# Down-projections of six of eight MLP stretches as seven block products, in a one-core hybrid decoder layer

## The chip, the cores and the metric

One Trainium2 chip, one of its cores. The metric is the device time of one execution in microseconds (us). The kernel before was timed three times: median 2252.41, from 2246.67 to 2255.57. The engines are TensorE (PE, matmuls), VectorE (DVE), ScalarE (ACT), GpSimd (POOL), and SyncE (SP), which only issues transfers.

## The reference

One layer for 1024 prompt tokens and 8 x 8 sample tokens (T = 1088 columns), model width 1024. A combined input projection feeds a retention branch and an RWKV-7 branch; their outputs are gated, merged and projected (`w_out`), then comes cross-attention, then the MLP, then a final norm. The change is about the MLP and about what prepares its weights:

```python
x = x + merged @ w_out
hq = _rmsnorm(x, g_cross)                     # cross-attention: w_cq, scores, softmax, values, w_co
x = x + ox @ w_co
hm = _rmsnorm(x, g_mlp)
x = x + jnp.square(jax.nn.relu(hm @ w_up)) @ w_down   # w_up 1024 x 4096, w_down 4096 x 1024
y = _rmsnorm(x, g_final)
```

## The kernel before, in words

**Number format.** Each weight and activation is held as a high part in fp32r and a remainder (the "low" part); one product is three matmul passes, high x high, high x low, low x high. For a weight tile POOL casts the high part and, in the projections, also subtracts to get the low part (`split`, L449 and L451). In the MLP POOL only casts (`pair`, L509) and DVE subtracts (`unit_lo`).

**Slots.** All weights lie in DRAM as slots of 128 x 1024, numbered: 14 RWKV slots from S_PW, 32 side slots, 8 branch-mix slots from S_MIX, 8 output-projection slots from S_OUT, 8 query slots, 8 slots of `w_co`, and then 64 MLP slots. SP loads a slot into a ring of two, POOL splits it, PE runs 72 matmuls on it. POOL's program is in the order of the slots; behind each of the first 32 splits it issues one DRAM-to-DRAM transfer (`sum_step`), which builds sums and differences of blocks of `w_up` in `sums_up` (a copy, `put`, or an adding transfer, `plus`), waiting on the semaphore `d_sum` of its group before it builds on an earlier one. SP waits for all of them before the first MLP load.

**MLP.** The hidden width is cut into 8 stretches of 512 columns, two to a group: group o = 0, then 1 and 2 in a hardware loop of two trips, then 3 (`pair_loop`); d = 0 or 1 is the stretch within the group. A stretch has two quads. A quad computes 256 hidden columns as seven block products (a Strassen-like scheme) over 2 x 2 blocks: token half, and input-row half or hidden-column half. Each product is a unit: one 256 KB load into the ring `mraw` of four, one cast, one low part, and 24 matmuls of 272 columns on two PSUM banks (`product`, issued through L517). ACT and DVE combine the accumulators in `hidf`, apply ReLU and the norm (`squeezed`), square on ACT (`squared`, a high part into `hid` and a full one into `hidf`), and DVE takes the low part (`hidden_lo`). After two quads the down-projection of these 512 hidden columns follows in the plain way: eight output tiles, each a unit of 36 matmuls (12 weight tiles x three column pieces of 364, 364 and 360) on three banks, and one addition of 1092 columns into the residual `F` by DVE (`down`).

**Order.** Every engine has its own program written out by hand, and semaphores tie them: `m_hi` and `m_ready` for the units' weights, `m_used` when PE has finished a unit, `m_lo` for the low parts of the hidden values, `m_f` for additions into `F`, `m_z`, `m_b`, `m_c` and `m_sq` for steps of a quad. DVE works strictly in order: within a quad its program is the list in `quad` of the vector block, in the first two quads that of `opening`. PE starts a down-projection when `m_lo` says that the low parts it reads are there; in the first stretch it waits for seven of the eight.

Of the kernel before, what the change touches and what calls it, by code (L numbers as in the profile page):

```python
# [30 lines left out]
ALU = mybir.AluOpType  # L31
# [92 lines left out]
def hybrid_step(nc, A):  # L124
    with ExitStack() as ctx:  # L125
# [40 lines left out]
        PAIR_UNITS = 44  # L166
# [8 lines left out]
        msp = at("msp", [P, 4, 2, 4, P], oW + 8192, F32R)  # L175
        Tn = at("Tn", [P, 4, TP], oA)
# [159 lines left out]
        m_p1, m_p5, m_hi, m_ready, m_used, t_sum = as_mx, as_ex, as_nm, as_tp, as_tc, as_ox  # L336
# [55 lines left out]
        sums_up = nc.dram_tensor("sums_up", (4, 4, 4, P, 4 * P), F32, kind="Internal").ap()  # L392
        C_CO = S_SIDE + 16 + 8 + 8
# [5 lines left out]
        def quad_unit(q):  # L399
            return 7 * q + 8 * (q // 2)  # L400

        def unit_of(first, q, p):
            return OPENING.index((q, p)) if first and q < 2 else quad_unit(q) + ORDER.index(p)

        OPENED = ((0, 0, 0), (1, 0, 0), (0, 0, 1), (1, 0, 1), (0, 1, 1), (1, 1, 1), (0, 1, 0), (1, 1, 0))

        def down_unit(d, t):
            return 14 + 22 * d + t

        def pair_loop(eng, body):  # L410

            body(0, 0, True, False)
            with eng.Fori(0, 2) as i:
# [3 lines left out]
        acc_a, acc_b, acc_c = ps[:, 0:2, 0:HC], ps[:, 6:8, 0:HC], ps[:, 3:5, 0:HC]  # L417

        ACC_OF = {1: acc_a, 2: acc_a, 3: acc_c, 5: acc_c, 4: acc_b, 6: acc_b, 7: acc_b}
        FIRST_ACC = [{1: acc_a, 2: acc_a, 5: acc_c, 3: acc_c, 6: acc_a, 7: acc_a, 4: acc_a},  # L420
                     {1: acc_a, 2: acc_a, 5: acc_b, 3: acc_b, 6: acc_c, 7: acc_c, 4: acc_c}]
# [19 lines left out]
        def _(pool):  # L441
# [23 lines left out]
            def put(g, kind, src):  # L465
                pool.dma_start(sum_block(g, kind), src).then_inc(d_sum[g], 16)

            def plus(g, kind, src):
                pool.dma_start(sum_block(g, kind), src, accum_op=ALU.add).then_inc(d_sum[g], 16)

            def sum_step(n):

                if n < 8:
                    put(n // 2, (S1, S3)[n % 2], up_block(n // 2, *(A21, A11)[n % 2]))
                elif n < 16:
                    g, j = (n - 8) // 2, n % 2
                    if j == 0:
                        pool.wait_ge(d_sum[g], 16 * 2)
                    plus(g, (S1, S3)[j], up_block(g, *(A22, A21)[j]))
                elif n < 32:  # L480
                    g, stage = n % 4, (n - 16) // 4
                    pool.wait_ge(d_sum[g], 16 * (4 + stage))
                    if stage == 0:
                        put(g, S2, sum_block(g, S1))
                    if stage == 1:
                        plus(g, S2, up_block(g, *A11))
                    if stage == 2:
                        put(g, S4, sum_block(g, S2))
                    if stage == 3:
                        plus(g, S4, up_block(g, *A12))  # L490

            for n in range(XT + SIDE):
                split(n, n % 2)
                if n < 32:
                    sum_step(n)
            with pool.Fori(0, (S_MLP - S_MIX) // 2) as i:
                for b in range(2):
                    split(i * 2 + (S_MIX - S_PW + b), b)

            def pair(i, o, first, last):  # L500

                for l in range(PAIR_UNITS):
                    pool.wait_ge(d_m[l % 4], i * 176 + (D_M + 176 * o + 16 * (l // 4) + 16))
                    if first and l < 4:
                        pool.wait_ge(g_done, C_CO + 7 + l // 2)
                    else:
                        pool.wait_ge(m_used, i * PAIR_UNITS + (BEFORE + PAIR_UNITS * o + l - 3))
                    pool.sem_inc(w_taken, 1)
                    pool.tensor_copy(msp[:, l % 4, 0, :, :], mraw[:, l % 4, :].rearrange("p (k n) -> p k n", k=4)).then_inc(m_hi, 1)  # L509
# [5 lines left out]
        def _(pe):  # L515
# [778 lines left out]
            def product(l, p, acc):  # L1294

                for k in range(4):
                    for m, (wp, xp) in enumerate(((0, 0), (0, 1), (1, 0))):
                        for c in range(2):
                            last = mm(acc[:, c, :], msp[:, l % 4, wp, k, :], X_OF[p][:, k, xp, HC * c:HC * c + HC],
# [3 lines left out]
            def opening():  # L1303
# [15 lines left out]
                for l, (q, p) in enumerate(OPENING):  # L1319
# [3 lines left out]
                    product(l, p, FIRST_ACC[q][p])  # L1323
# [3 lines left out]
            def quad(i, o, q):  # L1327

                n = 4 * o + q
                for p in ORDER:  # L1330
                    l = unit_of(False, q, p)
                    if p == 1:
                        pe.wait_ge(m_z, i * 16 + (BEFORE + 4 * n - 3))
                        if q % 2 == 0:
                            pe.wait_ge(m_f, i * 16 + (BEFORE + 4 * n - 1))
                    if p == 5:
                        pe.wait_ge(m_c, i * 4 + (BEFORE + n))
                        if q % 2 == 0:
                            pe.wait_ge(m_f, i * 16 + (BEFORE + 4 * n))
                    if p == 6:  # L1340
                        pe.wait_ge(m_b, i * 12 + (BEFORE + 3 * n))
                    if p == 2:
# [7 lines left out]
                    pe.wait_ge(m_ready, i * PAIR_UNITS + (BEFORE + PAIR_UNITS * o + l + 1))  # L1350
                    product(l, p, ACC_OF[p])

            def down_bank(t, c):
                return ps[:, 3 * (t % 2) + c, 0:real(c).stop - real(c).start]

            def down_part(l, t, ks):

                for k in ks:
                    for m, (wp, xp) in enumerate(((0, 0), (0, 1), (1, 0))):
                        for c in range(3):  # L1360
                            last = mm(down_bank(t, c), msp[:, l % 4, wp, k, :], hid[k // 2][:, k % 2, xp, real(c)],
                                      start=(k == m == 0), stop=(k == 3 and m == 2), skip=True)
                return last

            def down(i, o, first, d, tiles):

                z0, f0 = 16 * o + 8 * d, 16 * o + 8 * d
                for t in range(2):
                    l = down_unit(d, t)
                    pe.wait_ge(m_ready, i * PAIR_UNITS + (BEFORE + PAIR_UNITS * o + l + 1))  # L1370
                    if first and d == 0:
                        pe.wait_ge(m_lo, BEFORE + 7)
                        pe.wait_ge(m_b, BEFORE + 5 + t)
                    elif t == 0:
                        pe.wait_ge(m_lo, i * 16 + (BEFORE + z0 + 4))
                        pe.wait_ge(m_z, i * 16 + (BEFORE + 16 * o + 8 * d + 5))
                    else:
                        pe.wait_ge(m_c, i * 4 + (BEFORE + 4 * o + 2 * d + 2))
                    down_part(l, t, (0, 1))
                for t in range(2):  # L1380
                    if t == 0:
                        pe.wait_ge(m_lo, i * 16 + (BEFORE + z0 + 8))
                    down_part(down_unit(d, t), t, (2, 3)).then_inc(m_used, 1)
                for t in range(2, tiles):
                    l = down_unit(d, t)
                    pe.wait_ge(m_ready, i * PAIR_UNITS + (BEFORE + PAIR_UNITS * o + l + 1))
                    pe.wait_ge(m_f, i * 16 + (BEFORE + f0 + t - 1))
                    down_part(l, t, range(4)).then_inc(m_used, 1)

            def pair_of_groups(i, o, first, last):  # L1390

                for d in range(2):
                    if first and d == 0:
                        opening()
                    else:
                        quad(i, o, 2 * d)
                        quad(i, o, 2 * d + 1)
                    down(i, o, first, d, 6 if last and d == 1 else 8)
# [12 lines left out]
            for c in range(3):  # L1411
                n_c = ENDS[c].stop - ENDS[c].start
                for b in range(2):
                    l = down_unit(1, 6 + b)
                    if c == 0:
                        pe.wait_ge(m_ready, BEFORE + 3 * PAIR_UNITS + l + 1)
                        pe.wait_ge(m_f, BEFORE + 61 + b)
# [1611 lines left out]
```

## Time and profile before

| what | us |
|---|---|
| median of 3 runs | 2252.41 (2246.67 to 2255.57) |
| profiled execution, its own time | 2245.91 |
| its span, first to last instruction | 2244.1 |
| PE busy in it | 2182.6 (97%) |
| DVE busy | 1065.8 (47%) |
| ACT busy | 533.4 (24%) |
| POOL busy | 440.1 (20%) |
| mean granted TensorE clock | 0.996 |

Busy times are shares of the whole span. The MLP runs from 1489.8 us to the end of the span. A matmul's recorded length is longer than the distance between two matmul starts, since they overlap; the distance between starts of groups is what the groups cost.

### The profile page before, as it was taken

The numbers are of one execution on the slowest core, as the hardware profiler recorded it, in microseconds if no ns is written. First come the engines' busy times: TensorE is split into PE (matmuls) and PEld (weight loads), VectorE is DVE, ScalarE is ACT, GpSimd is POOL, SyncE is SP. The second block draws the span as 40 slices with busy tenths as digits, with TensorE's granted clock in tenths as the row PEclk, the third lists the DMA queues.
The fourth block names the chain that finished last, engine by engine and source line by source line (L and its number), as shares of the span: only waits on it lengthen the run. The fifth ranks groups of instructions, "written<-read, shape, count | busy, mean of one in ns | idle before, by whom it ended". The sixth has DMA issues, their size and how long they took to land. (4 is left out here: it accounts for less than half of the span.)

```text
span 2244.1 us, 49247 instructions
## 1 busy us (share of the span) xinstructions
PE 2182.6 (97%) x21418; PEld 2061.6 (92%) x21418; DVE 1065.8 (47%) x1526; ACT 533.4 (24%) x1014; POOL 440.1 (20%) x368
## 2 busy tenths in 40 slices
PE   8999999999999999999999999998999999999997
PEld 6899888888888899989999987998999999999997
DVE  5333643636445355263544155466445445354455
ACT  4111433324333221153011023231102011011023
POOL 0233301112021022122333200321111111111110
PEclk9999999999999999999999999999999999999999
DMA  8446513424053074336113125111212122122122
GB/s 306 144 129 137 142 39 82 89 54 149 7 114 70 27 244 162 105 135 254 47 40 119 47 96 187 38 57 62 70 53 76 57 67 72 52 76 64 55 76 80
DMA packets 86663, 217.61 MB, mean 97 GB/s; under 512 B 10720, under 2 KB 26464, under 8 KB 83680
## 3 DMA queue, kind: packets, MB, share of 16 engines
q1 hardware_dynamic: 62944, 156.22, 21.0%
q0 software_dynamic: 12800, 33.56, 6.9%
q10 hardware_dynamic: 10752, 25.35, 3.2%
q8 instruction: 137, 2.24, 0.4%
q14 instruction: 30, 0.25, 0.0%
HBM read 187.04 MB, written 61.60 MB: 111 GB/s over the span
## 5 line engine op out<-in xcount | busy, mean ns | idle before, releaser
L517 PE MATMUL ps<-A_s,w_split 128*128 128x364 f32 (+1 forms) x3888 | 693.5, 334 | 1.9 <-ACT zstg L2250 1.9
L517 PEld LDWEIGHTS ps<-A_s,w_split 128*128 128x128 f32 x3888 | 643.5, 188 | 28.1 <-issue 12.5
L517 PE MATMUL ps<-hid,msp 128*128 128x364 f32 (+3 forms) x2304 | 388.3, 330 | 5.4 <-issue 5.4
L517 PEld LDWEIGHTS ps<-hid,msp 128*128 128x128 f32 x2304 | 385.1, 189 | 7.3 <-issue 6.0
L449 POOL CAST w_split<-w_raw 128x1024 fp32r<-128x1024 f32 x78 | 85.5, 1096 | 1117.0 <-PE ps L517 858.0
L517 PE MATMUL ps<-B_s,w_split 128*128 128x364 f32 (+1 forms) x1728 | 288.1, 328 | 0.4 <-POOL w_split L451 0.4
L517 PEld LDWEIGHTS ps<-B_s,w_split 128*128 128x128 f32 x1728 | 286.7, 188 | 0.7 <-issue 0.7
L1434 DVE TENSOR_TENSOR F<-ps,F 128x1092 f32<-128x1092 f32 (+3 forms) x84 | 104.3, 1241 | 352.3 <-PE ps L517 352.3
L509 POOL CAST msp<-mraw 128x512 fp32r<-128x512 f32 x176 | 115.1, 655 | 616.6 <-PE ps L517 604.0
L451 POOL TENSOR_TENSOR w_split<-w_raw,w_split 128x1024 fp32r<-128x1024 f32 x78 | 206.9, 2652 | 6.3
L517 PE MATMUL ps<-xb,msp 128*128 128x272 f32 x1536 | 200.2, 288 | 1.5 <-DVE F L1434 1.5
L517 PEld LDWEIGHTS ps<-xb,msp 128*128 128x128 f32 x1536 | 195.9, 188 | 1.8 <-issue 1.8
L517 PE MATMUL ps<-xt,msp 128*128 128x272 f32 x1152 | 152.2, 288 | 1.5 <-DVE xt L1434 1.0
L517 PEld LDWEIGHTS ps<-xt,msp 128*128 128x128 f32 x1152 | 147.4, 188 | 2.1 <-DVE xt L1434 1.2
L1434 DVE TENSOR_TENSOR msp<-mraw,msp 128x512 fp32r<-128x512 f32 x176 | 121.2, 690 | 51.6 <-POOL msp L509 49.7
L2250 ACT ACTIVATE hidf<-ps 128x544 f32<-128x544 f32 x32 | 20.0, 626 | 383.2 <-PE ps L517 383.2
L1434 DVE TENSOR_TENSOR pdf<-prw 128x1024 f32<-128x1024 f32 x14 | 40.9, 2919 | 99.3 <-ACTq L2354 99.3
L2250 ACT ACTIVATE hid<-hidf 128x544 fp32r<-128x544 f32 x64 | 42.2, 660 | 190.9 <-DVE hidf L1440 190.9
L2250 ACT ACTIVATE zstg<-ps 128x364 f32<-128x364 f32 x96 | 45.3, 474 | 173.4 <-PE ps L517 130.0
L1434 DVE TENSOR_TENSOR hidf<-ps,hidf 128x544 f32<-128x544 f32 x62 | 44.9, 724 | 42.0 <-PE ps L517 42.0
L1434 DVE TENSOR_TENSOR Xst<-ps,msk 128x256 f32<-128x256 f32 (+1 forms) x88 | 35.8, 407 | 53.7 <-PE ps L517 52.0
L1434 DVE TENSOR_TENSOR F<-F 128x384 f32<-128x384 f32 (+2 forms) x64 | 43.9, 697 | 25.3 <-ACT F L2250 24.7
(249 smaller groups left out, 2408.4 us busy)
## 6 DMA issues: line engine op xcount, KB each, us to landing
w_raw<-w SPq DMA_DIRECT2D x80, 512.0 KB, 3.7
mraw<-w SPq DMA_DIRECT2D x112, 256.0 KB, 2.6
sums_up<-w POOLq DMA_DIRECT2D x24, 1024.0 KB, 9.4
mraw<-sums_up SPq DMA_DIRECT2D x64, 256.0 KB, 2.6
z<-zstg SPq DMA_DIRECT2D x83, 182.0 KB, 2.1
F<-z SPq DMA_DIRECT2D x16, 546.0 KB, 7.1
sums_up<-sums_up POOLq DMA_DIRECT2D x8, 1024.0 KB, 5.9
w_raw<-w SPq DMA_DIRECT2D x7, 1024.0 KB, 10.3
```

The source lines that it names most:

```text
L449: pool.tensor_copy(ws[:, b, 0, :, :], raw[:, b, :].rearrange("p (k n) -> p k n", k=KT)).then_inc(w_hi, 1)
L451: pool.tensor_tensor(ws[:, b, 1, :, :], raw[:, b, :].rearrange("p (k n) -> p k n", k=KT), w32, ALU.subtract).then_inc(w_ready, 1)
L509: pool.tensor_copy(msp[:, l % 4, 0, :, :], mraw[:, l % 4, :].rearrange("p (k n) -> p k n", k=4)).then_inc(m_hi, 1)
L517: return pe.matmul(out, lhsT, rhs, start=start, stop=stop, skip_group_check=skip)
L1434: return v.tensor_tensor(out, a, b, op)
L2250: return a.activation(out, in_, f, **k)
```

## The change

Six of the eight stretches (all but the first, o = 0 d = 0, and the last, o = 3 d = 1) do their down-projection as seven block products too. Output rows pair up (tiles 2t and 2t+1), tokens come in halves; each product takes two units u of 24 matmuls on 272 columns, so 14 units (`FAST`) of 336 matmuls, in place of 8 units of 288. Each unit's two tiles end separately (`m_half`, then `m_used`), and DVE adds or subtracts each into one block of `F` (`read`, 544 columns), 28 times a stretch. The residual is kept in a transformed form between: `residual_in` changes `F` once after the first down-projection and back before the last. Products need sums of blocks of the hidden values; they are made on DVE and ACT (`turned_hi`, `turned_lo`, `lower`, the scratch tile `tf`), partly in the second quad, partly between the reads.

Sums of `w_down` blocks are built in `sums_down` by 32 more steps of POOL's transfers: one per slot for n < 21 as before, two per slot for 21 <= n < 34, none until the output projection, then one per slot until all 64 are issued. The additions for groups 1 and 2 are two transfers each. The first stretch keeps its plain down-projection, but with another order of DVE's work at its end and PE starting on less (`down_first`). In quads, the accumulator of products 3 and 5 moves from banks 3 and 4 to 2 and 3.

```diff
-            for n in range(XT + SIDE):
+            for n in range(S_MLP - S_PW):
                 split(n, n % 2)
-                if n < 32:
-                    sum_step(n)
-            with pool.Fori(0, (S_MLP - S_MIX) // 2) as i:
-                for b in range(2):
-                    split(i * 2 + (S_MIX - S_PW + b), b)
+                for _ in range(1 if n < 21 else 2 if n < 34 else 0 if n < S_OUT - S_PW else min(1, 64 - done)):
+                    if done < 32:
+                        sum_step(done, 0, sum_block, up_block)
+                    else:
+                        sum_step(done - 32, 8, down_sum, down_block)
+                    done += 1
...
+            def plus(g, dst, src):
+                parts = [(dst[:, d], src[:, d]) for d in range(2)] if len(dst.shape) == 4 else [(dst, src)]
+                for x, y in parts:
+                    pool.dma_start(x, y, accum_op=ALU.add).then_inc(d_sum[g], 16)
...
+            def down_first():
+
+                r = [mlp_ring(0, down_unit(0, 0, t)) for t in range(2)]
                 for t in range(2):
+                    pe.wait_ge(m_ready, mlp_units(0, 0, down_unit(0, 0, t) + 1))
+                    pe.wait_ge(m_lo, mlp_lows(0, 0, 0, 2))
+                    pe.wait_ge(m_b, BEFORE + 5 + t)
+                    down_part(r[t], t, (0,))
+                for k, n in ((2, 4), (1, 6), (3, 8)):
+                    pe.wait_ge(m_lo, mlp_lows(0, 0, 0, n))
+                    for t in range(2):
+                        last = down_part(r[t], t, (k,))
+                        if k == 3:
+                            last.then_inc(m_used, 1)
...
+            OPERAND = {1: (0, 0), 2: (1, 0), 7: (0, 1), 3: (1, 1), 5: (0, 0), 4: (1, 0), 6: (0, 0)}
+            NEED = {1: 1, 2: 3, 7: 4, 3: 6, 5: 5, 4: 7, 6: 8}
+
+            def down_fast(i, o, d):
+
+                n = 4 * o + 2 * d + 2
+                for s, (p, u) in enumerate(FAST):
+                    l = down_unit(o, d, s)
+                    v, h = OPERAND[p]
+                    if u == 0:
+                        pe.wait_ge(m_lo, mlp_lows(i, o, d, NEED[p]))
+                    pe.wait_ge(m_ready, mlp_units(i, o, l + 1))
+                    for j in range(2):
+                        t = 2 * u + j
+                        if s >= 2:
+                            pe.wait_ge(m_f, mlp_reads(i, o, d, 4 * (s // 2 - 1) + t + 1))
...
+                        for k in range(2):
+                            for m, (wp, xp) in enumerate(((0, 0), (0, 1), (1, 0))):
+                                for c in range(2):
+                                    x0 = HT * h + HC * c
+                                    last = mm(ps[:, 2 * t + c, 0:HC], msp[:, mlp_ring(o, l), wp, 2 * j + k, :], hid[v][:, k, xp, x0:x0 + HC],
+                                              start=(p in (1, 7, 5, 6) and k == m == 0), stop=(k == 1 and m == 2), skip=p in (2, 3, 4))
+                        last.then_inc((m_half, m_used)[j], 1)
...
@@ vector: opening, its end @@
                 q0.c22()
+                unit_los(13, 14)
+                q1.c22()
                 lo(0)
-                lows(13)
-                lo(1)
-                q1.c22()
+                unit_los(15)
                 lo(2)
                 q0.c21()
-                lows(14)
+                q1.c21()
+                lo(1)
                 lo(3)
                 lo(4)
-                q1.c21()
-                lows(15)
+                unit_los(16)
+                lo(6)
                 lo(5)
-                lo(6)
-                lows(16)
+                unit_los(17)
                 lo(7)
-                lows(17)
...
@@ vector: quad; "odd" is the second quad of a stretch that is now fast @@
+                if odd:
+                    squares_of(i, z0)
+                    own.add(tt(tf, H11, H12, ALU.subtract))
                 unit_lo(i, o, l0 + 7)
                 c.c22()
-                hidden_lo(i, z0, q, 0, 0)
+                if odd:
+                    own.wait()
+                    lower(0, 0)
                 unit_lo(i, o, l0 + 8)
                 c.c12()
-                hidden_lo(i, z0 + 1, q, 1, 1)
+                if odd:
+                    hidden_lo(i, z0, q, 0, 0)
                 unit_lo(i, o, l0 + 9)
+                if odd:
+                    squares_of(i, z0 + 3)
+                    tt(H12, H12, H22, ALU.subtract).then_inc(t_sum, 1)
                 c.c21()
-                hidden_lo(i, z0 + 2, q, 0, 1)
                 unit_lo(i, o, l0 + 10)
-                hidden_lo(i, z0 + 3, q, 1, 0)
+                if alone or odd:
+                    hidden_lo(i, z0 + 3, q, 1, 0)
...
+            def down_fast(i, o, d):
+
+                for s, (p, u) in enumerate(FAST):
+                    l = down_unit(o, d, s)
+                    v.wait_ge(m_half, mlp_turns(i, o, d, 14, BEFORE + s + 1))
+                    read(p, 2 * u)
+                    v.wait_ge(m_used, mlp_units(i, o, l + 1))
+                    read(p, 2 * u + 1)
+                    unit_lo(i, o, l + 4)
+                    if s == 0:
+                        turned_lo(H12, 0, 1, mlp_turns(i, o, d, 4, BEFORE_R + 5))
+                    if s == 2:
+                        turned_lo(tf, 0, 0, mlp_turns(i, o, d, 4, BEFORE_R + 6))
+                    if s == 3:
+                        v.wait_ge(m_lo, mlp_lows(i, o, d, 5))
+                        own.add(tt(tf, H22, tf, ALU.add))
+                    if s == 4:
+                        own.wait()
+                        lower(1, 1)
+                    if s == 5:
+                        own.add(tt(H21_hi, f32(hid[1][:, :, 0, 0:HT]), tf, ALU.subtract))
+                    if s == 6:
+                        own.wait()
+                        tt(H21, H21_hi, f32(hid[1][:, :, 1, 0:HT]), ALU.add).then_inc(t_sum, 1)
+                    if s == 8:
+                        turned_lo(H21, 1, 0, mlp_turns(i, o, d, 4, BEFORE_R + 7))
+                    if s == 10:
+                        turned_lo(tf, 0, 0, mlp_turns(i, o, d, 4, BEFORE_R + 8))
```

## Rows read from the trace of the kernel before

**Rows 1.** The page: busy us of each engine, share of the span, instructions.

```profile
PE 2182.6 (97%) x21418; PEld 2061.6 (92%) x21418; DVE 1065.8 (47%) x1526; ACT 533.4 (24%) x1014; POOL 440.1 (20%) x368
```

**Rows 2.** Windows: stretch, length, busy us (instructions) per engine, clock, DMA share, GB/s.

```profile
1593.20:1614.30 21.10, 21.10 (x170) 21.10 (x169) 12.12 (x17) 4.87 (x8) 4.32 (x7) 1.00 0.24 75
1635.40:1683.30 47.90, 47.90 (x290) 47.90 (x289) 16.67 (x19) 1.21 (x2) 4.94 (x8) 1.00 0.17 50
```

**Rows 3.** Timeline of PE, a quad's begin and a down-projection: start us, us, what.

```profile
1593.23 6.19 PE L517 MATMUL ps<-xb,msp 128*128 128x272 f32 x48
1635.42 48.07 PE L517 MATMUL ps<-hid,msp 128*128 128x364 f32 x288
```

**Rows 4.** Timeline of PE in the first stretch; in brackets the idle time before.

```profile
1517.90 15.65 PE L517 MATMUL ps<-xt,msp 128*128 128x272 f32 x120 [0.98 <-DVE xt L1434]
1533.94 3.28 PE L517 MATMUL ps<-xt,msp 128*128 128x272 f32 x24 [0.38 <-DVE hidf L1434]
1542.59 50.81 PE L517 MATMUL ps<-hid,msp 128*128 128x364 f32 x288 [5.37 <-issue]
```

**Rows 5.** Windows around that idle time (the clock is third from the end).

```profile
1517.90:1533.90 16.00, 15.54 (x120) 15.13 (x120) 15.74 (x18) 4.77 (x8) 4.20 (x5) 1.00 0.24 70
1537.30:1542.50 5.20, 0.00 (x0) 0.00 (x0) 5.17 (x9) 2.07 (x4) 0.64 (x1) 0.92 0.16 54
1544.00:1546.00 2.00, 2.00 (x8) 2.00 (x7) 0.32 (x1) 0.00 (x0) 0.00 (x0) 0.50 0.64 203
1550.00:1552.00 2.00, 2.00 (x14) 2.00 (x14) 0.00 (x0) 0.00 (x0) 0.00 (x0) 1.00 0.00 0
```

**Rows 6.** Timeline of DVE before the first down-projection.

```profile
1526.13 2.42 DVE L1434 TENSOR_TENSOR xt<-xtf,xt 128x2176 fp32r<-128x2176 f32 x1
1528.47 1.10 DVE L1434 TENSOR_TENSOR msp<-mraw,msp 128x512 fp32r<-128x512 f32 x1
1529.49 0.71 DVE L1434 TENSOR_TENSOR hidf<-ps,hidf 128x544 f32<-128x544 f32 x1
...
1541.13 1.35 DVE L1434 TENSOR_TENSOR hid<-hidf,hid 128x544 fp32r<-128x544 f32 x2
```

**Rows 7.** Timeline of POOL in the same stretch, two casts.

```profile
1524.32 0.62 POOL L509 CAST msp<-mraw 128x512 fp32r<-128x512 f32 x1 [2.40 <-PE ps L517]
1527.33 1.69 POOL L509 CAST msp<-mraw 128x512 fp32r<-128x512 f32 x1 [2.40 <-PE ps L517]
```

**Rows 8.** Timeline of DVE over the end of a quad and a down-projection.

```profile
1725.72 0.72 DVE L1434 TENSOR_TENSOR hidf<-ps,hidf 128x544 f32<-128x544 f32 x1 [0.20 <-PE ps L517]
1726.48 0.72 DVE L1440 SCALAR_TENSOR_TENSOR hidf<-hidf,rsx 128x544 f32<-128x544 f32 x1
1727.12 0.72 DVE L1434 TENSOR_TENSOR hid<-hidf,hid 128x544 fp32r<-128x544 f32 x1
1727.76 0.68 DVE L1434 TENSOR_TENSOR msp<-mraw,msp 128x512 fp32r<-128x512 f32 x1
...
1734.71 1.29 DVE L1434 TENSOR_TENSOR F<-ps,F 128x1092 f32<-128x1092 f32 x1 [5.50 <-PE ps L517]
1735.92 0.68 DVE L1434 TENSOR_TENSOR msp<-mraw,msp 128x512 fp32r<-128x512 f32 x1
```

**Rows 9.** Timeline of ACT: the two squares of one hidden block.

```profile
1727.24 0.66 ACT L2250 ACTIVATE hid<-hidf 128x544 fp32r<-128x544 f32 x1 [1.72 <-DVE hidf L1440]
1727.81 0.64 ACT L2250 ACTIVATE hidf<-hidf 128x544 f32<-128x544 f32 x1
```

**Rows 10.** Timeline of POOL in the output projection: one split, and the next one's begin.

```profile
1100.03 1.04 POOL L449 CAST w_split<-w_raw 128x1024 fp32r<-128x1024 f32 x1 [7.37 <-PE ps L517]
1101.15 2.40 POOL L451 TENSOR_TENSOR w_split<-w_raw,w_split 128x1024 fp32r<-128x1024 f32 x1
1111.95 1.04 POOL L449 CAST w_split<-w_raw 128x1024 fp32r<-128x1024 f32 x1 [8.41 <-PE ps L517]
```

**Rows 11.** The weight sums' transfers on POOL: ns min/median/max of an issue.

```profile
L469 POOL DMA_DIRECT2D sums_up<-w x16: 1243/1257/1278, 157.1 to 684.7; - x16
```

**Rows 12.** The page's DMA issues: KB each, us from issue to landing.

```profile
mraw<-w SPq DMA_DIRECT2D x112, 256.0 KB, 2.6
sums_up<-w POOLq DMA_DIRECT2D x24, 1024.0 KB, 9.4
```

More of the change, by code:

```diff
@@ L1322, in opening @@
                     pe.wait_ge(m_ready, BEFORE + l + 1)
[L1323 removed]
+                    product(mlp_ring(0, l), p, FIRST_ACC[q][p])
                     if l == 1:
@@ L1360, in down_part @@
                         for c in range(3):
-                            last = mm(down_bank(t, c), msp[:, l % 4, wp, k, :], hid[k // 2][:, k % 2, xp, real(c)],
-                                      start=(k == m == 0), stop=(k == 3 and m == 2), skip=True)
-                return last
-            def down(i, o, first, d, tiles):
-                z0, f0 = 16 * o + 8 * d, 16 * o + 8 * d
+                            last = mm(G[t % 2][:, c, 0:real(c).stop - real(c).start], msp[:, r, wp, k, :],
+                                      hid[k // 2][:, k % 2, xp, real(c)], start=(k == m == 0), stop=(k == 3 and m == 2), skip=True)
@@ L2201, in pair_of_groups, with residual_in @@
+            F12, F21, F22 = F[:, 0:8:2, HT:T], F[:, 1:8:2, 0:HT], F[:, 1:8:2, HT:T]
+            def residual_in(n, op1, op2):
+                v.wait_ge(m_f, n)
+                own.add(tt(F12, F12, F22, op1))
+                own.add(tt(F21, F21, F22, op2))
+                own.wait()
             def pair_of_groups(i, o, first, last):
@@ L2205, in pair_of_groups @@
                         opening()
-                    else:
-                        quad(i, o, 2 * d)
-                        quad(i, o, 2 * d + 1)
-                    down(i, o, d, 6 if last and d == 1 else 8, last)
-            QUAD_STEPS = 1
+                        down(0, 0, 8)
+                        continue
+                    quad(i, o, 2 * d)
+                    if first:
+                        residual_in(mlp_reads(0, 0, 1, 0), ALU.add, ALU.subtract)
+                    if last and d == 1:
+                        residual_in(mlp_reads(0, 3, 1, 0), ALU.subtract, ALU.add)
+                    quad(i, o, 2 * d + 1)
+                    if mlp_fast(o, d):
+                        down_fast(i, o, d)
+                    else:
+                        down(3, 1, 6)
+            PAIR_STEPS = 10
             pair_of_groups(0, 0, True, False)
-            with v.Fori(0, 2) as i, own.loop(i, 2, 4 * QUAD_STEPS):
+            with v.Fori(0, 2) as i, own.loop(i, 2, PAIR_STEPS):
                 pair_of_groups(i, 1, False, False)
```

308 lines of the change are left out of this document (199 added, 109 removed).

## The prediction

> **What bounds the kernel.** I read the busy shares first, then the windows of the MLP by stage, then PE's timeline, and last the order of DVE's work. The shares say that PE is busy 97% of the span and DVE 47% [rows 1], so a gain has to be PE time, and DVE's mean says nothing until it is read stage by stage. The windows say that PE has no gap in a steady quad or in a steady down-projection, at the full clock [rows 2]. The reader should see there how differently the two load DVE: 12.12 of 21.1 us in the first quad, 16.67 of 47.9 us in the down-projection. The only long stop of PE in the MLP is 5.37 us ahead of the first down-projection [rows 4], and behind it the clock is at half speed for a while [rows 5].
>
> **The matmuls.** A unit of 24 matmuls on 272 columns: a quad of seven takes 21.1 us [rows 2], so 3.014 us a unit, 125.6 ns a matmul (the two units of 48 that open a quad are recorded with 6.19 [rows 3], start to end). A plain down-projection is 288 matmuls of about 364 columns in 47.9 us [rows 2, 3], 166.3 ns each. A fast one is 14 units of the quad's shape, with the same weight loads per matmul: 14 x 3.014 = 42.2 us. The difference is 5.7 us a stretch, 34.3 us for six. That is the ceiling of this part, and it holds only if DVE delivers in time.
>
> **DVE in a fast stretch.** Durations overlap a little, so I take distances between starts: 0.64 us for 544 columns, 0.76 where the next depends on it, about 0.61 for a unit's low part, 1.21 for 1092 columns [rows 8], which I take for the 1088-column operations too. A fast stretch gives DVE 28 reads (28 x 0.64 = 17.9), 14 unit low parts (14 x 0.61 = 8.5) and eight operations of 1088 columns (9.7): 36.1 us of 42.2. The mean would fit. The order does not: in units s = 2 to 6 DVE has 1.28 + 0.61 + 1.21 = 3.1 us in each 3.014 us unit, and it does not come in with an empty queue. In the second quad the sum H12 - H22 stands ahead of the last read and waits for ACT's square of the third block (two passes, 0.57 + 0.64 [rows 9]), and the last low part waits for the square of the fourth. Walking the queue from these rows, with 0 at the start of the stretch on PE: third block squeezed at -1.1, its square at 0.2, H12 - H22 until 1.4, last read of the quad at 1.4 (in the kernel before 0.2 after the end of the unit [rows 8]), its squeeze, one unit low part, and the last hidden low part at 4.2 to 4.9. The first two products' reads begin at 4.9 instead of 1.7. From there nothing is idle: the low part of the turned block at 6.75, tile reads until 9.1 where PE wants the bank at 9.04, and `lower(1, 1)`, the sixth low part, ends at about 19.2. PE wants it for product 3, unit 6, at 18.1. So PE waits 1.2 us once a stretch. After unit 6 DVE has slack (of the seven units left two carry an operation of 1088 columns) and I find no second wait; the weights' loads are a ring of four with 12 us to land in 2.6 [rows 12].
>
> One thing makes it worse. When a DVE operation with two inputs in SBUF meets a cast of POOL, one of them is held: the cast beside the 2176-column operation took 1.69 us instead of 0.62, and the low part behind it 1.10 instead of 0.68 [rows 6, 7, 8]. In the steady quad before, the cast falls beside a read of PSUM and costs nothing. With DVE late by 2 us, the casts meet 1088-column operations. The cost is 0.42 each time; two such meetings lie ahead of the sixth low part, but part of the second is hidden, so I take 0.5, and the wait becomes 1.7 us. The Trainium skill, page "GPSIMD Engine Reference", section "Key points", says that GpSimd shares its SBUF interfaces with VectorE and contends with DVE instructions that have two SBUF inputs. By that rule the reads of PSUM stay free and the turned operations pay; without it the wait would be 1.2. The trace agrees, by the 0.42 us.
>
> Bounds of the wait: no operation of 1088 columns with these inputs stands in the trace. Below, it is gone if they take some 1.1 us and ACT's squares come earlier: 0 to 0.3. Above, if every unit ahead of the sixth low part pays a meeting of 0.42, it is 3 us. I take 1.7: six stretches, 10.2 us. Net of the six: 34.3 - 10.2 = 24.1 us.
>
> **Clock.** An idle PE of 0.98 us left the clock at 1.00 and one of 5.37 us was followed by 0.50 [rows 4, 5]. A wait of 1.7 is nearer to the first; I cost it without a fall.
>
> **The quads.** The first quad of a stretch loses four low parts of hidden blocks (4 x 0.64) on DVE, the second gains 3 x 1.21 less 2 x 0.64. DVE was at 12.12 of 21.1 us in the first [rows 2], so both fit. `residual_in` is two operations of 2176 columns, 2.42 us each [rows 6], between two quads where DVE has over 1.5 us idle in most units: its late low parts are two units ahead of their use, so 0, at worst 1 us, twice. The bank moves cost nothing: the reads that now free them come one unit before.
>
> **The opening.** Before, PE waits 5.37 us for seven low parts, then runs its first 27 matmuls in about 7.2 us where the steady rate gives 4.5 (288 took 50.81 until their end, against 48.07 in steady state [rows 3, 4]): 2.7 us for the half clock [rows 5]. After, the read for unit 13 is ahead of the low parts: DVE reaches it at about 1532.6, so PE starts that unit at 1533.4, 0.5 us earlier, and ends it at 1536.4. The first down matmuls need two low parts and the read of c21: at 1537.0 by the same walk, 0.6 us idle. Then one tile's first quarter until 1538.5, the other's until 1540.0, 0.4 us of waiting for the fourth low part, and with 18 matmuls (3.0 us) a step the sixth and eighth come in time. The first two tiles end at 1549.4 and six more at 5.99 each: 1585.4, where the trace has 1593.2. Gain 7.8 us, less 0.1 because tile 0's read is now 1.5 us before its bank is wanted: 7.7. Bounds: 3 (PE starts three us later than I walk, and the clock falls as before) and 8.5 (all of 5.37 + 0.38 + 2.7).
>
> **The weight sums.** 40 more transfers, 24 MB, on POOL behind the splits. In the output projection a slot is 11.92 us, of which POOL uses 1.12 + 2.40 [rows 10], so about 8 us are free. An issue was 1.26 us for 512 rows of 2 KB, and 0.7 ahead of it [rows 11]; rows of 1 KB are twice as many, so at most 2.5 us an issue, 5 for a split addition: hidden. A step waits for the step four before it of its group, two slots back in the late RWKV slots and four in the projections, at 11.92 us or more a slot 24 and 48 us, against 9.4 to land [rows 12]: no wait. In the RWKV slots the bytes double for eight slots; some loads may be late. Bounds 0 and 3 us, I take 0.5. SP's wait ahead of the MLP is met: the last step is issued at slot 70, some 100 us before.
>
> **Sum.** -24.1 - 7.7 + 0.5 = -31.3 us. Against the profiled execution, 2245.9 us, that is 2214.6. It lies 6.5 us under the median of the runs shown (2252.4, lowest 2246.7), so against the median it is 2221.
>
> **Rivals.**
> Forecast, PE's new matmuls with one DVE wait a stretch: 2221, on its own 2214 to 2229. Chance 0.56.
> No DVE wait: 34.3 + 7.7 - 0.5 = 41.5 less, 2211. For it: mean load of 36.1 in 42.2. Against: the sixth low part has to be 1.2 us faster. Chance 0.13.
> The opening gains nothing (another low part or a bank is late and the clock falls all the same): 23.6 less, 2229. Chance 0.08.
> DVE becomes the bound of the fast stretches: each wait reaches 3 us, 2229; and if it is long enough for the clock to fall, 2.7 us more, so 5.7 a stretch and all of the 34.3 is gone: 2245. For it: five units running at 3.1 us of DVE work and the casts' meetings. The Trainium skill, "TensorE: Matmul & The Clock Gate", Part 1, says that an idle array is set back to half rate; the rows show it after 5.37 us. Chance 0.16, of it half near 2229 to 2238.
> The slower one: POOL is held by its transfers. If a down step keeps POOL beyond the 8 us that a slot leaves (descriptors of 1 KB rows, or `d_sum` waits), every split behind is late and PE stops. From 8 us it costs, at 10.5 us it costs 2.5 in each of some 17 slots of the projections, 42 us, against 31 gained: 2263. Against it: the issue of 1.26 us. Chance 0.07.
>
> A measurement can tell about 0.5%, 11 us, from no change. Faster by more: the first three and half of the fourth, 0.84; within: 0.09; slower: 0.07. Range for 8 in 10: 2208 to 2237.
>
> **What would show it.** PE timeline: fast stretches of 14 units in 43.9 us with one idle time of 1.7 us at unit 6, released by DVE's write of `hid`. Unit 6 without idle: the no-wait rival. Waits at other units released by `F`: DVE is the bound. The windows of fast stretches with DVE above 36 us busy and clock 1.00. The first down-projection starts near 1537 with no half clock behind it. POOL's issues in the output projection under 3 us, and no wait of PE on `w_split`. The forecast is wrong if PE's idle time in the six stretches is above 20 us or below 4.

## The result, and the profile after

The changed kernel ran in 2239.75 us (median of 4, 2239.52 to 2245.65) beside 2251.17 for the kernel before: ratio 0.995, 95% interval 0.9926 to 0.9973. That is 11.4 us, where 31.3 was forecast, and outside the range. The profiled execution has a span of 2243.7 us; the three others of the changed kernel are 6 us shorter, so the profile shows all of the loss and some more. The profiled execution of the kernel before is 5.3 us under its median, which makes the lateness read from the two traces larger once more.

The first lines of the page of the changed kernel (columns as in [rows 1], then the transfers by queue):

```profile
PE 2165.4 (97%) x21706; PEld 2039.3 (91%) x21706; DVE 1201.1 (54%) x1716; ACT 553.0 (25%) x1026; POOL 528.0 (24%) x444
...
q0 software_dynamic: 27840, 58.72, 13.2%
```

PE's busy time fell by 17.2 us, its matmuls rose by 288, and the queue of POOL's transfers carries 58.72 MB. Now PE's timeline: the norm's sums that stand near the beginning of the MLP, the first down-projection, and the first two fast stretches:

```profile
1522.22 2.15 PE L564 MATMUL ps<-T,ones 128*128 128x512 f32 x6 [0.65 <-DVE T L1529]
...
1562.67 3.38 PE L564 MATMUL ps<-hid,msp 128*128 128x364 f32 x18 [0.48 <-DVE hidf L1529]
1566.26 45.38 PE L564 MATMUL ps<-hid,msp 128*128 128x364 f32 x270 [0.21 <-DVE hid L1529]
1653.67 18.29 PE L564 MATMUL ps<-hid,msp 128*128 128x272 f32 x144
1673.48 24.57 PE L564 MATMUL ps<-hid,msp 128*128 128x272 f32 x192 [1.52 <-DVE hid L1529]
1740.08 18.23 PE L564 MATMUL ps<-hid,msp 128*128 128x272 f32 x144
1760.49 24.83 PE L564 MATMUL ps<-hid,msp 128*128 128x272 f32 x192 [2.18 <-DVE hid L1529]
```

The norm's sums stood at 1496.64 in the kernel before:

```profile
1496.64 2.15 PE L517 MATMUL ps<-T,ones 128*128 128x512 f32 x6 [0.66 <-DVE T L1434]
```

So the MLP begins 25.6 us late, and everything behind it is 26.0 us shorter (2243.7 - 1522.22 against 2244.1 - 1496.64). The MLP gained most of what was forecast, and the part before it, costed at 0.5 us, took it back. PE's waits over the span name what is new there:

```profile
PE ps L564 <- issue: 11.3, 7, 2.9
PE ps L564 <- DVE hid L1529: 10.8, 7, 2.2
```

The second row is the DVE queue of the fast stretches. The first is time in which PE waited for nothing that the profile shows; it was 8.6 us in five pieces before, 5.4 of them ahead of the first down-projection [rows 4], and that piece is gone. Of the 11.3 us now, 8.1 lie between 700 and 790 us, in four pieces, where the kernel before (from 695 to 782) has 0.8.

Where the 25.6 us arise is read from POOL's casts, one for each slot, set against the kernel before: 1.6 us late at slot 21, 6.8 at slot 22 (3.4 at the next), 6.9 at slot 31, 16.3 at slot 32, 19.4 at slot 33, 25.5 at slot 40, and constant from there to the MLP. POOL's timeline from slot 31 to slot 32:

```profile
687.20 1.04 POOL L479 CAST w_split<-w_raw 128x1024 fp32r<-128x1024 f32 x1 [6.39 <-issue]
688.32 2.59 POOL L481 TENSOR_TENSOR w_split<-w_raw,w_split 128x1024 fp32r<-128x1024 f32 x1
691.65 1.28 POOL L501 DMA_DIRECT2D sums_down<-w  x1 [0.73 <-POOL w_split L481]
700.16 1.25 POOL L501 DMA_DIRECT2D sums_down<-w  x1 [7.23 <-issue]
709.61 1.26 POOL L501 DMA_DIRECT2D sums_down<-w  x1 [8.20 <-issue]
710.36 1.55 POOL L479 CAST w_split<-w_raw 128x1024 fp32r<-128x1024 f32 x1
```

An issue is recorded with 1.26 us, as before [rows 11]. But another one behind it does not start for 7 to 8 us more. The last two of the three are the two halves of one addition, with no semaphore between them, and they stand 9.45 us apart. The next split came at 710.4; 701 is where it would have been if slot 32 were as late as slot 31.

### The profile page after: what moved, and what is told of

Its sections match the earlier page's. It is cut to its first block and busy times, and to the rows that moved or that the text cites. A ratio compares the mean times of both kernels' runs of the same rounds, so it can differ in the third digit from the quotient of the medians.

```text
span 2243.7 us, 50369 instructions
## 1 busy us (share of the span) xinstructions
PE 2165.4 (97%) x21706; PEld 2039.3 (91%) x21706; DVE 1201.1 (54%) x1716; ACT 553.0 (25%) x1026; POOL 528.0 (24%) x444
## 3 DMA queue, kind: packets, MB, share of 16 engines
q0 software_dynamic: 27840, 58.72, 13.2%
## 5 line engine op out<-in xcount | busy, mean ns | idle before, releaser
L564 PE MATMUL ps<-hid,msp 128*128 128x272 f32 (+4 forms) x2592 | 357.5, 299 | 11.2 <-DVE hid L1529 10.8
L564 PEld LDWEIGHTS ps<-hid,msp 128*128 128x128 f32 x2592 | 351.7, 189 | 16.2 <-issue 10.3
L556 POOL CAST msp<-mraw 128x512 fp32r<-128x512 f32 x212 | 163.7, 773 | 542.7 <-PE ps L564 530.0
L1529 DVE TENSOR_TENSOR msp<-mraw,msp 128x512 fp32r<-128x512 f32 x212 | 149.8, 709 | 56.7 <-POOL msp L556 53.9
L1529 DVE TENSOR_TENSOR F<-ps,F 128x1092 f32<-128x1092 f32 (+3 forms) x36 | 42.0, 1168 | 161.0 <-PE ps L564 161.0
L1529 DVE TENSOR_TENSOR F<-F,ps 128x544 f32<-128x544 f32 x168 | 115.1, 713 | 22.0 <-PE ps L564 21.1
L2424 ACT ACTIVATE hid<-hidf 128x544 fp32r<-128x544 f32 (+1 forms) x64 | 47.6, 744 | 287.2 <-DVE hidf L1535 173.2
L1529 DVE TENSOR_TENSOR F<-F 128x384 f32<-128x384 f32 (+3 forms) x68 | 52.0, 777 | 25.3 <-ACT F L2424 24.8
```

The source lines that it names most:

```text
L556: pool.tensor_copy(msp[:, r, 0, :, :], mraw[:, r, :].rearrange("p (k n) -> p k n", k=4)).then_inc(m_hi, 1)
L564: return pe.matmul(out, lhsT, rhs, start=start, stop=stop, skip_group_check=skip)
L1529: return v.tensor_tensor(out, a, b, op)
L2424: return a.activation(out, in_, f, **k)
```

## The experiments

The three theories at the start were these. Theory 1: POOL is held at an issue while earlier transfers are in its queue, and splits come late. Theory 2: the bytes slow other traffic wherever they fall. Theory 3: bunching any sums costs. All kernels below ran beside the kernel before on the same chip; ratios are against it, with 95% intervals. One trace is a rough measure of lateness: seven kernels whose POOL programs are alike up to slot 46 (a_nodown, the four of the a_spread family, a_out and a_out_lo2) are 2.3 to 12.2 us late there against the one trace of before.

**Only the sums, on the kernel before.** b_sums has the new list of steps in POOL's block and nothing else of the change.

> The kernel before with POOL's whole new list of weight sums (64 steps, in the order and at the slots of the change), the down sums built and never read. If the sums are what ate the gain, this is 18 to 26 us slower than before: 2269 to 2277. If they are cheap, as the prediction had it, it is within 3 us of before and the loss has another place.

2264.7 against 2249.2 us, ratio 1.0071 (1.0052 to 1.0090): 15.5 us slower, a little under the stated window. Slot 32 is 17.2 us late in it. The loss is in the sums, apart from the rest of the change.

**Only the up sums bunched.** `for _ in range(1 if n < 21 else 2 if n < 34 else 0)` with 32 steps.

> The kernel before with the 32 up sums alone, but two per slot from n = 21. In the trace after, slot 22 was 5 us late and got 2 of them back. If bunching any two transfers behind a split costs time, 3 to 5 us slower: 2255. If only the new down sums cost, within 1 us of before.

2250.9 us, 1.0007 (0.9990 to 1.0023): no change that can be told. Slot 22 was late by 8.5 us in its trace and the next by 2.0: a late split is made up where PE has RWKV work to do meanwhile. As the price of 15.5 us theory 3 is out; the 3 to 5 us that the text above gives it are not excluded, since the interval reaches 5 us. The trace shows one thing more, that the hold is no new property of the down sums. Two additions of the up sums (1024 KB in 512 rows of 2 KB), which the kernel before never issues one behind the other, stand 9.6 us apart here, and two others 12.4 us (404.67 and 417.06):

```profile
528.21 1.27 POOL L469 DMA_DIRECT2D sums_up<-w  x1 [0.74 <-POOL w_split L451]
537.81 1.25 POOL L469 DMA_DIRECT2D sums_up<-w  x1 [8.34 <-issue]
```

The first transfer of each pair landed 9.3 and 12.1 us after its issue, so the second started 0.3 us behind the landing of the first.

**The change without down sums.**

```diff
-                for _ in range(1 if n < 21 else 2 if n < 34 else 0 if n < S_OUT - S_PW else min(1, 64 - done)):
+                for _ in range(1):
                     if done < 32:
                         sum_step(done, 0, sum_block, up_block)
-                    else:
-                        sum_step(done - 32, 8, down_sum, down_block)
-                    done += 1
+                        done += 1
```

> The changed kernel without the down sums; the up sums one per slot as before, and the units that read a down sum read a block of the up sums in its place, so the down-projections compute other values. All else as changed. MLP part of the prediction: 24.1 + 7.7 us under before, 2219; by the MLP of the trace after (25.3 us shorter) 2225. If the sums are not the loss: 2240.

2225.2 us, 0.9898 (0.9874 to 0.9922): 24.1 us under before, where the trace after had said 2225 and the prediction's terms 2219. This is the price of the sums in the change: 14.6 us between the two medians, and 12.7 us if each is set against the kernel before that ran beside it (24.1 less 11.4).

**The same bytes in long rows.** `down_block` takes whole rows of one or two slots (4 KB) in place of quarter rows.

> The changed kernel, its down sums with the same number of transfers, the same bytes and the same slots, but each in rows of 4 KB in place of 1 KB (other weights are added up, so the down-projections compute other values). Theory 1, POOL is held at an issue until the rows of the transfers ahead have been taken off its queue: a quarter of the rows, POOL is held little, 2222 to 2228. Theory 2, the bytes delay the other traffic: unchanged, 2240. Theory 3, POOL is held for each transfer whatever its rows: unchanged, 2240, with the same gaps between POOL's issues.

2230.9 us, 0.9918 (0.9894 to 0.9943): 9 of the 14.6 us are gone (6.9 of the 12.7). Its POOL issues stand back to back, four in 3.32 us, and slot 32 is no later than slot 31 (3.7 us both):

```profile
701.87 3.32 POOL L501 DMA_DIRECT2D sums_down<-w  x4 [0.66 <-POOL w_split L481]
```

So the hold goes with the number of rows, not with the number of transfers or the bytes: additions of 512 rows hold POOL at 1 KB and at 2 KB a row, additions of 128 rows do not at 4 KB. This is theory 1, with rows. Rows are not all of it, for two plain copies of 512 rows do go out together (b_put32 below, 700.50 us, two issues in 1.56 us). And from slot 32 to 33, where no split is due for 73 us, this kernel still loses 5.3 us.

**Other slots, first try.** None from slot 32 until the branch-mix slots, then one step per slot, the last seven behind slot 71 (I meant them to lie under cross-attention).

> The changed kernel with the weight sums at other slots: one step per slot for n < 32 (the up sums, as in the kernel before), none until the branch-mix slots, then one per slot for the down sums, and the last seven steps behind the first slot of w_co, under cross-attention. Theory 1 (POOL held at issues delays splits in RWKV, where two transfers follow one split): the loss in RWKV is gone, and in the projections a held POOL has 8 us to spare: 2223 to 2228, near the kernel without down sums (2225.2). Theory 2 (the bytes cost wherever they fall): 2237 to 2240.

2271.4 us, 1.0098 (1.0079 to 1.0116): a miss by 45 us, and a clear one. Split 71 itself comes only after the attention, so seven steps stood between it and split 72, and PE waited 34.6 us:

```profile
1441.05 1.25 POOL L501 DMA_DIRECT2D sums_down<-w  x1 [6.80 <-issue]
1449.03 1.25 POOL L501 DMA_DIRECT2D sums_down<-w  x1 [6.73 <-issue]
1457.27 1.26 POOL L501 DMA_DIRECT2D sums_down<-w  x1 [6.98 <-issue]
1465.38 1.25 POOL L501 DMA_DIRECT2D sums_down<-w  x1 [6.85 <-issue]
1466.13 1.55 POOL L479 CAST w_split<-w_raw 128x1024 fp32r<-128x1024 f32 x1
```

```profile
1470.23 59.98 PE L564 MATMUL ps<-B_s,w_split 128*128 128x364 f32 x343 [34.59 <-POOL w_split L481]
```

The distance between issues, 8.0 to 8.2 us here and up to 9.45 in the trace after, is the price that the prediction lacked. A split addition is 16 us, longer than a slot of 11.95: from slot 57 to 61 four of them in a row made PE late by about 10 us more. The rest of this family is compared with a_spread only.

**DVE's order in the fast stretch.** Two edits, one after the other.

```diff
                     read(p, 2 * u + 1)
-                    unit_lo(i, o, l + 4)
+                    if s not in (3, 4):
+                        unit_lo(i, o, l + 4)
...
                         lower(1, 1)
+                        unit_lo(i, o, l + 3)
+                        unit_lo(i, o, l + 4)
```

> a_spread, with the unit low parts of units s = 3 and 4 of a fast stretch moved behind lower(1, 1), so DVE reaches the sixth low part 1.2 us sooner. If PE's wait at unit 6 is the DVE queue as walked, it falls from 1.4 to 2.2 us to 0.2 to 1.0, 7 us less than a_spread in six stretches: 2218. If the wait comes from ACT or from the operand itself, no change.

2264.5 us, 7.0 less than a_spread, as the walk had it. The wait at unit 6 is 0.3 to 0.6 us, and a small one of 0.3 us appears four units later.

The second edit puts `H12 - H22` behind `c.c21()` and its unit low part.

> a_spread_lo, with H12 - H22 behind the last read of the second quad and not ahead of it. The walk gives the last hidden low part 0.8 us sooner and the rest of the queue with it: PE's wait at unit 6 is gone or under 0.3 us, 1 to 3 us less than a_spread_lo: 2216. If another DVE operation then binds, no gain.

2257.2 us, 7.2 less again, where 1 to 3 were expected. A fast stretch is now without a gap:

```profile
1764.16 42.79 PE L564 MATMUL ps<-hid,msp 128*128 128x272 f32 x336
```

In the traces, too, the part from the norm's sums to the end is 7.0 us shorter (716.4 and 709.3 us). The waits that are gone, two in each fast stretch, were 4.4 us in all; the forecast had left out the second one of each stretch. Where the other 2.6 us come from was not looked into.

**The opening as before**, on a_spread.

> a_spread with the opening as in the kernel before (DVE's order of low parts, PE waiting for seven of them). The prediction's term for the opening: 7.7 us slower than a_spread, 2233, with an idle time of about 5.4 us and a half clock behind it. If the new opening had saved only the idle time and not the clock, 5 us.

2275.7 us, 4.3 more than a_spread. From the norm's sums to the first fast stretch its trace has 137.8 us and a_spread's 131.4: 6.4 us for the opening, of 7.7 forecast. The idle time of 5.36 us is back, and its down-projection takes 49.80 us instead of 50.81 [rows 4], so less is lost behind the idle time here: 1.0 of the 1.3 us between forecast and trace.

**The repairs of DVE's order on the change itself** (a_lo2, both edits, sums as changed).

> The changed kernel, its weight sums as they are, with the two changes of DVE's order alone. If the DVE queue and the sums are two separate losses they add: 14 us less than the changed kernel, 2226.

2226.4 us, 0.9886 (0.9864 to 0.9907), beside 2253.9 for before: as expected. PE's wait on `hid` is 0.2 us in total, and from the norm's sums to the end its trace is 13.8 us shorter than the trace after. The gain of DVE's order is there with the sums as they are: the DVE queue and the sums are two losses that add.

**Single transfers.** Up sums one per slot; the first eight copies behind slot 32; one transfer, never both halves, behind each of slots 48 to 69; the last ten behind slot 70, ahead of cross-attention.

> The changed kernel with the down sums' transfers one by one where POOL has time: the up sums one per slot for n < 32; the first eight copies behind slot 32, whose next split is 73 us later; then a single transfer per slot (never two halves) from slot 48 to 69; the last ten behind slot 70, whose next split comes only after cross-attention. Theory 1 (a POOL transfer of 1 KB rows holds the next issue for about 8 us; what costs is only a hold longer than the distance to the next split): as cheap as no down sums at all, 2225 to 2228. Theory 2 (the bytes cost wherever they fall): 2237 or more.

> a_single with both changes of DVE's order (unit low parts of s = 3, 4 behind lower(1, 1); H12 - H22 behind the last read of the second quad). With PE's six waits gone, about 14 us less than a_single (1.9 of wait and 0.4 of smaller waits a stretch, and 1.5 of half clock in two of them): 2212. It should beat the kernel before by 1.6% and the changed one by 1.2%.

2236.1 us, 0.9919 (0.9902 to 0.9935), and 2223.1 us, 0.9880 (0.9859 to 0.9900). Splits are up to 4.8 us late at slots 49 to 51, but PE waits only 0.6 us for one; the projections and the attention come at no cost, and still 11.8 us are lost between slots 32 and 33. The repair of DVE's order is worth 13 us again. Both lie 8 to 11 us above their expectation, so theory 1 is not all. In that stretch (695 to 782 us) these are PE's waits:

```profile
PE ps L580 <- issue: 9.2, 5, 3.4
PE ps L580 <- DVE Sst L1548: 1.7, 7, 0.3
```

The longest one is followed by matmuls at half clock for some us (granted 0.66 in the window 730 to 735):

```profile
727.26 0.28 PE L580 MATMUL ps<-Sst,G0T 64*64 64x64 f32 x4
730.99 0.39 PE L580 MATMUL ps<-QT,Sst 64*64 64x64 f32 x4 [3.45 <-issue]
```

**The same eight copies at two places**, on the kernel before. Theory A: transfers of POOL's queue in flight stop PE itself where it issues tiny matmuls densely. Theory B: only late splits cost. Neither kernel has a split due.

```diff
+                if n == 32:
+                    for k in range(8):
+                        g = k // 2
+                        pool.dma_start(down_sum(g, (S1, S3)[k % 2]), down_block(g, *(A21, A11)[k % 2])).then_inc(d_sum[g], 16)
```

> The kernel before plus only eight of the down sums' copies (6 MB in rows of 1 KB, never read), back to back behind slot 32 in RWKV; the next split is 73 us later, so POOL's hold delays no split. Theory A (POOL's transfers in flight delay PE itself while it issues many tiny matmuls; the trace of a_single has five stops of PE there for which it waited on nothing shown): 6 to 11 us slower. Theory B (only a late split costs): no change.

> The same eight copies, back to back behind slot 70, under cross-attention, where PE issues a third as many matmuls in a microsecond, and POOL again has no split to do for 98 us. Theory A: under 2 us. If transfers cost wherever they fall: 6 to 11 us slower as the other.

Behind slot 32: 2258.5 us, 1.0043 (1.0027 to 1.0059), 8.5 us over 2250.0. Behind slot 70: 2251.0, 1.0003 (0.9992 to 1.0014). The windows of b_put32, and of the kernel before from slot 32 to 33:

```profile
694.00:776.00 82.00, 72.51 (x2172) 64.59 (x2172) 31.71 (x76) 21.75 (x56) 10.35 (x10) 0.92 0.36 98
```

```profile
694.00:767.30 73.30, 68.66 (x2204) 60.54 (x2202) 32.22 (x78) 22.38 (x60) 3.43 (x2) 1.00 0.06 18
```

About the same matmuls in 8.7 us more, with the clock at 0.92; PE's stops on nothing shown are 6.4 us in six pieces, 2.1 at the longest. This is b_put70 beside the eight copies:

```profile
1297.00:1345.00 48.00, 46.87 (x350) 40.40 (x353) 25.24 (x55) 15.68 (x56) 6.92 (x8) 1.00 0.75 237
```

There are 350 matmuls in 48 us and no such stop, although the transfer engines are busier: 0.75, against 0.55 over the copies in b_put32 (700 to 744 us). So transfers in flight cost PE time at one place and not at the other; theory B and theory 2 in its general form are out. The two places differ in how densely PE issues, as theory A says, but in other things too, so that the density is the reason is argued and not shown.

**None beside RWKV.** One transfer per slot from 46 to 69, five behind slot 66, and the last twelve behind slot 70: eight additions and the four copies between them, not eight transfers as the text below has it. Then the same with DVE's order.

> a_single with the first eight copies moved out of RWKV too: single transfers from slot 46 to 69 and the last eight behind slot 70. Nothing of the down sums falls beside RWKV. Theory A: as the kernel without down sums, 2225 to 2228, 8 to 10 us less than a_single. Theory B: the same as a_single, 2236.

> a_out with both changes of DVE's order: the two repairs together. 13 to 14 us less than a_out: 2212 to 2214, 1.7% under before.

2235.4 us (2229.0 to 2239.6), 0.9924 (0.9907 to 0.9941), and 2219.3 us, 0.9862 (0.9843 to 0.9880). The first is 8 us above what theory A gave and lands on theory B's number. The traces tell why that does not save theory B. Between slots 32 and 33, where a_single lost 11.8 us, the two lose 1.5 us and nothing, as theory A has it. But they lose 3.2 and 1.6 us between slots 46 and 51, and 7.6 and 6.4 us between slots 70 and 71, under attention, where a_single with its ten transfers lost nothing. There PE waits for the attention's keys, 4.3 us in the first and 3.6 in the second, and the clock falls behind it (0.81 in the window 1330 to 1340 of the first):

```profile
1337.01 1.94 PE L580 MATMUL ps<-kc,qz 128*32 128x256 f32 x16 [4.30 <-DMA kc<-kc]
```

The transfers of the keys landed after 4.6 to 6.2 us in the kernel before and after up to 12.7 us here, so in this place POOL's transfers did delay the other traffic, as theory 2 says. The rest of the first one's distance is there already at slot 46: it is 7.1 us late, and its twin with the other DVE order, the same up to there, 3.0.

The second has the lowest median of all, 30.7 us under its before, 5 us above its expectation. It can't be told from a_single_lo2 (30.8 under its before), and the intervals of both meet that of a_lo2, which leaves the sums where the change had them (27.6 under). So what was won back is DVE's order, 13 us; moving the sums gave some 3 us more once that was repaired. An estimate for both repairs and no down sums at all is 24.1 + 13 = 37 us under before, so some 6 us of the sums' price are still paid.

## Why the prediction was wrong

The step that failed is the term "The weight sums", in its words "at most 2.5 us an issue, 5 for a split addition: hidden" and "Bounds 0 and 3 us, I take 0.5". It measured 15.5 us by itself (b_sums), 12.7 to 14.6 in the change (against a_nodown), 25.6 in the one profiled execution. Two things stood in place of it. First, I took the recorded length of a lone issue [rows 11] for what a transfer holds POOL. The rows of before hold none that follow another within its landing time of 9.4 us [rows 12], so they could not show the hold of 8 us; the bound had to reach up to the landing time, which gives 19 us for a split addition, over the 8 us that a slot leaves. (The doubling "rows of 1 KB are twice as many" does not hold for a half of an addition either: it has 512 rows, as many as a transfer of an up sum.) For the same reason the sign that was named, "POOL's issues in the output projection under 3 us", is met with 1.26 us and says nothing; the distance between two issues is what shows the hold. The rival of a held POOL had the right mechanism with a chance of 0.07; it put the place in the projections, where the hold cost nothing in the change (slots 61 to 63 were late by up to 6.8 us, and PE waited 0.7 us), while in RWKV, where three transfers followed one split, it did. Second, PE itself stops while such transfers run beside RWKV, with its dense tiny matmuls, 8.5 us for eight copies; no part of the text had it. How the 12.7 to 15.5 us divide between the two was not measured.

The other terms, by their own steps:

- **The matmuls.** Right: gapless, a fast stretch is recorded with 42.5 to 42.8 us (42.2 forecast), in the a_spread_lo2 trace.
- **DVE in a fast stretch.** Right in place, cause and size for the first stretch. Forecast from its start at 1653.67: last hidden low part 4.2 to 4.9, first reads at 4.9, PE held until 19.8. In the trace below: 4.1 to 4.8, 4.7, and PE goes on at 19.81.

```profile
1657.76 0.72 DVE L1529 TENSOR_TENSOR hid<-hidf,hid 128x544 fp32r<-128x544 f32 x1 [0.67 <-ACT hidf L2424]
1658.40 1.35 DVE L1529 TENSOR_TENSOR F<-F,ps 128x544 f32<-128x544 f32 x2
1659.66 0.69 DVE L1529 TENSOR_TENSOR msp<-mraw,msp 128x512 fp32r<-128x512 f32 x1
1660.26 1.70 DVE L1529 TENSOR_TENSOR hid<-hidf,hid 128x1088 fp32r<-128x1088 f32 x1
...
1672.15 1.27 DVE L1529 TENSOR_TENSOR hid<-hidf,hid 128x1088 fp32r<-128x1088 f32 x1
```

  The six waits are 1.39 to 2.18 us, 10.5 in all (10.2 forecast; 4 to 20 was the sign for being right). The meetings with POOL's casts show: 1.70 us for the turned low part instead of 1.27, and casts of 1.71 and 1.79 us instead of 0.62.
- **Clock.** Half wrong. The stretch whose wait was 2.15 us had the clock at half for 4 us and took 26.32 us where others took 24.8; one with 2.18 us kept it. These are the windows behind the wait of 2.15 us:

```profile
1936.00:1938.00 2.00, 1.74 (x8) 1.74 (x9) 2.00 (x5) 0.00 (x0) 0.00 (x0) 0.61 0.26 82
1938.00:1940.00 2.00, 2.00 (x11) 2.00 (x10) 1.83 (x2) 0.00 (x0) 0.00 (x0) 0.54 0.36 79
1940.00:1942.00 2.00, 2.00 (x18) 2.00 (x17) 0.84 (x2) 0.00 (x0) 0.62 (x1) 1.00 0.14 52
```

  In the trace of a_spread waits of 2.17 and 2.18 us were both followed by a fall (26.30 and 26.32 us), so the length alone does not decide it. With smaller waits inside the stretches this makes the six stretches' gain 18.0 us instead of 24.1 (from 1653.67 to 2177.96, against 1635.42 to 2177.75).
- **The opening.** Right: PE begins the down-projection at 1562.67, which is 1537.1 on the clock of before (1537.0 forecast), with waits of 0.48 and 0.21 us, and ends it at 1585.9 (1585.4). Gain 7.3 us, forecast 7.7; no half clock.
- **The quads and `residual_in`.** Right, 42.2 us for two quads after as before, 0 us.

So the sum was -24.1 - 7.7 + 0.5, and the profiled execution has -18.0 - 7.3 + 25.6 = +0.3 where its span is 0.4 us shorter. Of the 0.7 us between, 0.6 lie behind 2177.96, in the last stretch, which is unchanged (65.7 us, 66.4 before).

## What to carry to other kernels

A queue that is idle between its transfers in a trace says nothing on how close they can stand: when a change puts two behind one another on an engine that also has work to do, take the first one's landing time for the hold (here the second started 0.3 us behind it), not the recorded length of an issue, and let a step that others wait for never stand behind two. Put background transfers where the next piece of that engine's work is far away, away from dense tiny matmuls, and count what else loads there: the same eight copies cost 8.5 us beside RWKV and 1 us or nothing beside attention, but twelve transfers beside attention went with keys that came 4 us late. And an engine with a mean load of 36 in 42 us can still be the one that PE waits for: walking its queue in program order from a few durations gave the mean wait to 0.1 us (1.7 and 1.76), and moving three operations removed it, 13 us.

## What the runs showed of the hardware

- An adding transfer on POOL's queue of 512 KB in rows of 1 KB lets the next one start 8.0 to 9.5 us after its own start (a_spread, after), and one of 1024 KB in rows of 2 KB 9.6 to 12.4 us (b_bunch); with the 512 KB in rows of 4 KB four issues take 3.32 us (a_rows4k). A copy of 1024 rows of 1 KB holds the next one 7.5 to 7.7 us, and two copies of 512 rows go out together (b_put32). What in its queue is used up by rows was not looked into.
- PE, at some 26 matmuls in a microsecond, most of them on 64 columns, stopped up to 3.45 us at a time for nothing that the profile shows while POOL's transfers ran (a_single; 2.1 us in b_put32), and at 7 in a microsecond did not (b_put70). That its instructions arrive late behind these transfers would fit, since the page lists queues of instructions (q8 and q14) among those of the 16 transfer engines; no run separated that from another cause, so it stays open.
- A wait of PE of 2.15 us was followed by half clock and one of 2.18 us was not (after); in a_spread one of 2.18 us was. None of 1.39 to 1.72 us was followed by it in these traces.
